# First block: the second gate's sums on ScalarE and GpSimd, and tile 0 normed, queried and routed ahead of tile 1

## What is computed

```python
mod = c_act @ w_ada[l] + b_ada[l]
shift1, scale1, gate1, shift2, scale2, gate2 = split(mod, 6)
h = rms_norm(x, norm1_g[l]) * (1 + scale1) + shift1
mix = concat(attention(h), conv(h), pool(h)) @ w_out[l]
x = x + gate1 * mix
h2 = rms_norm(x, norm2_g[l]) * (1 + scale2) + shift2
# peer_ffn(h2): 8 heads; q = h2 @ w_q; scores of 2 x 128 keys; top 16 of the sums;
# for each token and head 16 rows of peer_u and 16 rows of peer_v are gathered
x = x + gate2 * peer_ffn(h2, peer_wq[l], peer_keys[l], peer_u[l], peer_v[l])
```

## Time and profile before

| | us or share |
|---|---|
| median of three executions | 2767.92 |
| the profiled execution's own time | 2766.92 |
| its span in the profile | 2765.2 |
| TensorE matmul busy | 2401.3 (87%) |
| VectorE busy | 2048.1 (74%) |
| ScalarE busy | 770.8 (28%) |
| GpSimd busy | 1056.0 (38%) |
| bytes moved by DMA | 812.71 MB, mean 294 GB/s |

### The profile page before, as it was taken

One profiled execution on the slowest core, in us unless ns is written; L12 is line 12 of the kernel. 1 busy time (PEld: TensorE's weight loads), 2 busy tenths in 40 slices (PEclk: granted clock), 3 DMA queues, 4 the chain that ended last, 5 costly groups with the idle time before them and its releaser, 6 DMA issues. The chain is left out here.

```text
span 2765.2 us, 31596 instructions
## 1 busy us (share of the span) xinstructions
PE 2401.3 (87%) x9946; PEld 1612.3 (58%) x9946; DVE 2048.1 (74%) x3778; ACT 770.8 (28%) x1088; POOL 1056.0 (38%) x1144
## 2 busy tenths in 40 slices
PE   6979877787778989777778778999999999998998
PEld 5666333333335775333333336888878898887787
DVE  7877788787787876778778777667777656655765
ACT  3422011011012322101100114446543444345443
POOL 1336777777772336777777770002000000000000
PEclk9989998888889999999989889999999999999999
DMA  9789999999999789999999997664466655652564
GB/s 354 253 315 367 409 410 410 409 409 410 410 401 345 253 301 365 409 410 410 409 409 410 410 401 222 195 181 120 141 177 191 191 161 175 190 175 69 158 184 137
DMA packets 424192, 812.71 MB, mean 294 GB/s; under 512 B 26024, under 2 KB 262130, under 8 KB 424094
## 3 DMA queue, kind: packets, MB, share of 16 engines
q0 software_dynamic: 147968, 537.84, 49.2%
q1 hardware_dynamic: 276126, 273.62, 31.3%
HBM read 810.32 MB, written 1.05 MB: 293 GB/s over the span
## 5 line engine op out<-in xcount | busy, mean ns | idle before, releaser
L1833 PE MATMUL ps<-weight_ring,arena 128*128 128x512 f32 x1616 | 810.3, 661 | 254.6 <-PEq L1830 152.2
L1833 PEld LDWEIGHTS ps<-weight_ring,arena 128*128 128x128 f32 x1616 | 339.1, 214 | 720.6 <-issue 720.6
L2577 DVE CUSTOM_DVE_ANT_0 arena<-arena,ps 128x1024 f32<-128x1024 f32 x384 | 455.8, 1218 | 164.5 <-DMA arena<-in_peer_u,expert 145.4
L1466 PE MATMUL ps<-hT_pair,w_hi 128*128 128x512 f32 x1312 | 461.5, 396 | 7.4 <-PEq L1860 7.2
L2137 DVE TENSOR_TENSOR ring_lo<-weight_ring,w_hi 128x3072 fp32r<-128x3072 f32 (+1 forms) x102 | 325.4, 3191 | 172.0 <-DVEq L2136 171.9
L759 POOL DMA_INDIRECT weight_ring<-in_peer_v,expert x390 | 373.0, 956 | 121.2 <-issue 69.6
L753 POOL DMA_INDIRECT arena<-in_peer_u,expert x360 | 341.8, 949 | 134.9 <-issue 54.0
L1465 PE MATMUL ps<-hT_pair,ring_lo 128*128 128x256 f32 x1148 | 320.7, 279 | 0.0
L1466 PEld LDWEIGHTS ps<-hT_pair,w_hi 128*128 128x128 f32 x1312 | 240.8, 188 | 57.1 <-issue 10.1
L921 ACT ACTIVATE w_hi<-weight_ring 128x3072 fp32r<-128x3072 f32 (+1 forms) x102 | 267.7, 2626 | 8.8 <-ACTq L920 8.7
L1130 ACT ACTIVATE acts<-dots 128x8 f32<-128x8 f32 x64 | 13.2, 209 | 865.9 <-ACTq L1129 865.8
(11 more groups left out here) (404 smaller groups left out, 3943.6 us busy)
## 6 DMA issues: line engine op xcount, KB each, us to landing
weight_ring<-in_w_ada SPq DMA_DIRECT2D x48, 1024.0 KB, 7.5
weight_ring<-in_ffn_w_gate SPq DMA_DIRECT2D x88, 512.0 KB, 4.0
weight_ring<-in_ffn_w_up SPq DMA_DIRECT2D x88, 512.0 KB, 5.3
weight_ring<-in_ffn_w_down SPq DMA_DIRECT2D x88, 512.0 KB, 5.8
weight_ring<-in_peer_wq SPq DMA_DIRECT2D x16, 1024.0 KB, 9.6
weight_ring<-in_w_in SPq DMA_DIRECT2D x14, 1024.0 KB, 7.7
weight_ring<-in_rg_w_in SPq DMA_DIRECT2D x12, 896.0 KB, 5.2
weight_ring<-in_w_out SPq DMA_DIRECT2D x8, 1024.0 KB, 7.5
```

Of the source, the lines that this page charges most:

```text
L1466: ins = mm(both, w_high, s_pair, start=(k == 0), stop=last)
L1833: ins = mm(ps[:, 2 * t + c, :], diag[:, k, :], v_place(l, k)[:, c * N:(c + 1) * N], start=False, stop=False, skip_group_check=True)
L2577: ins = v.tensor_tensor_reduce(out=row, in0=row, in1=h_rows(t), scale=1.0, scalar=0.0, op0=ALU.mult, op1=ALU.add, accum_out=dots[:, g, j:j ...
```

## The change

- GATE2's eight partial sums leave VectorE. ScalarE scales the eight half pieces in place (Copy with a scale), GpSimd adds them up with eight `tensor_tensor` of 128x1024. GpSimd now raises `ada_free[q]` and `bias_free` of this segment. ScalarE's loop stands ahead of its copy of the spread SHIFT2.
- On VectorE tile 0 is added, normed and its head 0 routed (`best_pairs`) before tile 1 is added and normed. `next_first` goes 1 after `add_gated(0)`, 3 after tile 0's norm, 1 after `add_gated(1)`, 3 and 4 after tile 1's norm, 4 at the end. `slot_free[3]` is raised after `best_pairs(0)`.
- On TensorE `out_rows(3, 1)` moves behind `first_head(0)`; the spread of GATE2 waits for GpSimd; the spread of the next SCALE1 moves behind `query(1)`.
- On ScalarE tile 1's mean square moves behind `first_head(0)`, and writes its squares to `h` instead of the scratch `junk`.

```diff
--- before.py
+++ after.py
@@ -404,6 +404,8 @@
         gates_ready, root_in, root_ready = sem("gates_ready"), sem("root_in"), sem("root_ready")
         gelu_ready, rnn_out_ready = sem("gelu_ready"), sem("rnn_out_ready")
         wf_ready = sem("wf_ready")
+        gate2_in = [gates_ready, root_in, root_ready, gelu_ready]
+        gate2_bias_in, gate2_scaled, gate2_ready = rnn_out_ready, exp_ready, abs_ready
         zeroed_for_act = sem("zeroed_for_act")
         f_by_head, f_turned = qk_done, qk_turned
         f_ready, log_f_ready = sem("f_ready"), sem("log_f_ready")
@@ -482,8 +484,8 @@
                 sp.sem_inc(free, -1)
                 sp.dma_start(gain[:], A[name][l:l + 1].to_broadcast([P, D])).then_inc(given, 16)
 
-            def bias_row(l, segment, pad):
-                sp.dma_start(pad[0:1, :], A["b_ada"][l:l + 1, segment * D:(segment + 1) * D]).then_inc(bias_in, 16)
+            def bias_row(l, segment, pad, given=bias_in):
+                sp.dma_start(pad[0:1, :], A["b_ada"][l:l + 1, segment * D:(segment + 1) * D]).then_inc(given, 16)
 
             def segment_bias(l, segment):
                 sp.wait_ge(bias_free, 1)
@@ -552,9 +554,14 @@
                 segment_bias(l, SHIFT2)
                 for u in range(4):
                     later_piece(l, SHIFT2, u)
-                segment_bias(l, GATE2)
+                sp.wait_ge(bias_free, 1)
+                sp.sem_inc(bias_free, -1)
+                bias_row(l, GATE2, bias_pad, gate2_bias_in)
                 for q in range(ADA_PAIRS):
-                    later_piece(l, GATE2, q)
+                    sp.wait_ge(ada_free[q], 1)
+                    sp.sem_inc(ada_free[q], -1)
+                    src = A["w_ada"][l].rearrange("(p k) n -> p k n", k=KC)
+                    sp.dma_start(ada_piece(SLOTS + q), src[:, 2 * q:2 * q + 2, GATE2 * D:(GATE2 + 1) * D]).then_inc(gate2_in[q], 16)
                 w_q = of("peer_wq").rearrange("(k p) n -> p k n", p=P)
                 if l + 1 < DEPTH:
                     load_gain(l + 1, "norm1_g", gain_pre, pre_in, pre_free)
@@ -742,6 +749,22 @@
                     pool.wait_ge(pool_steps, steps.next())
                 pool.sem_inc(pool_steps, -steps.reset())
                 g.tensor_tensor(pooled[:], pooled[:], zc[:, 6:8, :], ALU.subtract).then_inc(pooled_ready, 1)
+
+                gate2 = mod[:, GATE2, :]
+                pool.wait_ge(gate2_bias_in, 16)
+                pool.sem_inc(gate2_bias_in, -16)
+                for q in range(ADA_PAIRS):
+                    for k in range(2):
+                        pool.wait_ge(gate2_scaled, 1)
+                        pool.sem_inc(gate2_scaled, -1)
+                        g.tensor_tensor(gate2, ada_piece(SLOTS + q)[:, k, :], bias_pad[:] if q == 0 and k == 0 else gate2,
+                                        ALU.add).then_inc(pool_steps, 1)
+                        pool.wait_ge(pool_steps, steps.next())
+                    pool.sem_inc(ada_free[q], 1)
+                    if q == 0:
+                        pool.sem_inc(bias_free, 1)
+                pool.sem_inc(gate2_ready, 1)
+                pool.sem_inc(pool_steps, -steps.reset())
 
 
                 chosen_by = [expert[:, 0, :], expert[:, 1, :], first_expert]
@@ -1065,11 +1088,15 @@
                 a.activation(mixT[:, 0:4, P:SEQ], ps[:, 2, :].rearrange("p (c t) -> p c t", t=P), ACT.Copy).then_inc(mixT_ready, 1)
                 a.activation(table_use[:], eps[:], ACT.Sqrt).then_inc(act_steps, 1)
                 act.wait_ge(act_steps, steps.next())
+                for q in range(ADA_PAIRS):
+                    act.wait_ge(gate2_in[q], 16)
+                    act.sem_inc(gate2_in[q], -16)
+                    for k in range(2):
+                        piece = ada_piece(SLOTS + q)[:, k, :]
+                        a.activation(piece, piece, ACT.Copy, scale=c_act[:, 2 * q + k:2 * q + k + 1]).then_inc(gate2_scaled, 1)
                 spread(mod[:, SHIFT2, :], 2)
                 norm_x_tile(0)
                 evacuate_hT_tile(0, hT, WORK)
-                norm_x_tile(1)
-                act.sem_inc(act_steps, -steps.reset())
 
                 def first_head(t):
 
@@ -1088,6 +1115,8 @@
                             fan(act, key_s_ready)
 
                 first_head(0)
+                norm_x_tile(1, h[:, 1, :])
+                act.sem_inc(act_steps, -steps.reset())
                 spread(mod[:, GATE2, :], 2)
                 evacuate_hT_tile(1, hT, WORK)
                 first_head(1)
@@ -1580,10 +1609,10 @@
                 pe.wait_ge(attn_done, 2)
                 pe.sem_inc(attn_done, -2)
 
-            def spread(source, bank, give, alone=True):
-
-                pe.wait_ge(segment_ready, 1)
-                pe.sem_inc(segment_ready, -1)
+            def spread(source, bank, give, alone=True, ready=segment_ready):
+
+                pe.wait_ge(ready, 1)
+                pe.sem_inc(ready, -1)
                 for c in range(2):
                     ins = mm(ps[:, bank + c, :], ones[:], source[:, c * N:(c + 1) * N], start=alone, stop=True)
                 ins.then_inc(give, 1)
@@ -1743,7 +1772,6 @@
                 out_rows(1, 1).then_inc(slot_free[1], 1)
                 spread(mod[:, SHIFT2, :], 2, spread_for_act)
                 out_rows(2, 1).then_inc(slot_free[2], 1)
-                out_rows(3, 1, stop=True)
 
                 def weights_in(head):
 
@@ -1777,11 +1805,10 @@
                 pe.sem_inc(spread_taken, -1)
                 w_first = weights_in(0)
                 first_head(0, w_first)
-                spread(mod[:, GATE2, :], 2, spread_for_act)
+                out_rows(3, 1, stop=True)
+                spread(mod[:, GATE2, :], 2, spread_for_act, ready=gate2_ready)
                 turn_h_tile(1, WORK)
                 first_head(1, w_first)
-                if l + 1 < DEPTH:
-                    spread(mod[:, 0, :], 6, spread_for_dve)
                 job = 4
 
                 def query(head):
@@ -1811,6 +1838,8 @@
                     job += 1
 
                 query(1)
+                if l + 1 < DEPTH:
+                    spread(mod[:, 0, :], 6, spread_for_dve)
                 for head in range(2, EXPERT_HEADS):
                     query(head)
                     key_products(head - 1)
@@ -2451,15 +2480,12 @@
                 while parts:
                     next_part()
                 more = l + 1 < DEPTH
-                later_part(0, mod[:, GATE2, :])
                 dve.wait_ge(post_in, 16)
                 dve.sem_inc(post_in, -16)
                 scaled_gain(mod[:, SCALE2, :], 0, gain_post[:])
                 dve.sem_inc(spread_taken, 1)
                 if l + 1 == DEPTH:
                     dve.sem_inc(post_free, 1)
-                for q in range(1, ADA_PAIRS):
-                    later_part(q, mod[:, GATE2, :])
                 take_mod()
                 first_parts = [(q, k, segment) for segment in (SCALE1, SHIFT1) for q in range(ADA_PAIRS) for k in range(2)] if more else []
 
@@ -2485,16 +2511,14 @@
                             if q == ADA_PAIRS - 1:
                                 dve.sem_inc(segment_ready, 1)
 
-                for t in range(TILES):
-                    dve.wait_ge(rows_done, 1)
-                    dve.sem_inc(rows_done, -1)
-                    if t == TILES - 1:
-                        dve.sem_inc(slot_free[SLOTS - 1], 1)
-                    add_gated(t, GATE1, h_rows)
-                    next_first(1)
-                    if t == 0:
-                        take_mod()
-                    normalise_tile(t, mod[:, SCALE2, :], mod[:, SHIFT2, :])
+                dve.wait_ge(rows_done, 1)
+                dve.sem_inc(rows_done, -1)
+                add_gated(0, GATE1, h_rows)
+                next_first(1)
+                take_mod()
+                normalise_tile(0, mod[:, SCALE2, :], mod[:, SHIFT2, :])
+                next_first(3)
+
                 def best_keys(s, scored=half_s):
 
                     v.max(best[:, s, 0:8], scored[:, s, :]).then_inc(dve_steps, 1)
@@ -2558,14 +2582,21 @@
                     head_scored()
                     best_keys(s, key_s[:, 0])
                 best_pairs(0, first_expert[:])
+                dve.wait_ge(rows_done, 1)
+                dve.sem_inc(rows_done, -1)
+                dve.sem_inc(slot_free[SLOTS - 1], 1)
+                add_gated(1, GATE1, h_rows)
+                next_first(1)
+                normalise_tile(1, mod[:, SCALE2, :], mod[:, SHIFT2, :])
                 if more:
-                    next_first(6)
+                    next_first(3)
+                    next_first(4)
                     dve.wait_ge(pre_in, 16)
                     dve.sem_inc(pre_in, -16)
                     scaled_gain(gain_pre[:], 6, gain_pre[:])
                     dve.sem_inc(spread_taken, 1)
                     dve.sem_inc(u_free, 1)
-                    next_first(8)
+                    next_first(4)
                     assert not first_parts
```

## The result

The kernel after took 2794.84 us (median of four executions, 2787.99 to 2797.32), beside 2770.22 for the kernel before (four executions, 2764.54 to 2775.84): a ratio of 1.0089, with a 95% interval from 1.0075 to 1.0102. It is slower by 24.6 us. The prediction was 2789, in a range from 2776 to 2797.

A forecast was written before the change was run, and what follows sets the result against it. The prediction took TensorE's row of queries, which opens the last gate before DMA saturates, as the bound. Layer 1's 15.4 plus layer 0's 5.6 made 21.0 us on 2766.92, 2787.9; the median runs 1.0 higher: 2789, range 2776 to 2797.

The forecast's parts named there:

- TensorE's row of queries: Claimed bound: query(1) plus the later heads' queries opens the last gate before DMA saturates, not the first gather.
- The rival that the first gather sets the end: The end moves with the first gather, -3.3 us at best in each layer: 2761, or 2768 if collisions eat it; chance 0.10.
- TensorE's two waits: Layer 0, heads 5 and 6: TensorE waited 1.13 us and about as much again; later queries needn't, 2.3 us less.
- the late case: Layer 0 with queries later than before: TensorE needn't wait for heads 5 and 6, 2.3 us less.
- Tile 0 in layer 1: Tile 0's norm ahead of tile 1 on VectorE: 3.3 us gained at best, 2.3 lost to collisions, a gain of 1.0.
- the collisions: GpSimd's adds and VectorE's two-input sums make each other wait while tile 0 is added and normed: 2.3 us lost.
- the 3.3: Layer 1: tile 0 normed at 976.05 us at the earliest, against 979.35, a gain of 3.3 us at best.
- Tile 0 in layer 0: The gain of 1.0 less 2.0 us of waiting for the next SCALE1's first piece: a loss of 1.0 us.
- Tile 1 behind the routing: Tile 1's uncovered chain delays query(1): 8.83 us from add_gated to first_head's first matmul, then 9.0 for first_head(1).
- The sum: Later queries cost +15.4 us in layer 1 and +5.6 in layer 0, 21.0 together: 2789.
- The loads behind slot_free[3]: Layer 0: weights of heads 6 and 7 land 5.2 us later than the gates allow: +26.3 us, 2794; chance 0.17.

The follow-up runs named there:

- the order alone: The kernel after, but with GATE2's eight sums left on VectorE, so only the order changes: 2790.43 us, ratio 1.0086 to the kernel before.
- the rows ahead: New order, GATE2's sums on VectorE, but tile 1's last output rows stay ahead of tile 0's turn on TensorE: 2789.46 us, ratio 1.0072 to kernel before.
- spread alone: The kernel before with only the spread of the next SCALE1 moved behind query(1), in layer 0: 2770.25 us, ratio 1.0002.

## Why the prediction was right, and where it was not

**What sets the end.** "The last gate opens by TensorE's row of queries" is shown for layer 1: by the table, and by the delayed query(1). The rival that the first gather sets the end fell there. For layer 0 it is true of the kernel after: TensorE had no wait for weights from query(1) to the last head, and h stands 57.62 us behind query(1), to 0.01 us as in the order alone and with the rows ahead. It is not true the other way round: queries earlier than those of the kernel before meet the loads and gain nothing (spread alone). The prediction saw TensorE's two waits there, but used them only for the late case. For a change that only made things later, that did no harm.

**Tile 0 in layer 1, forecast a gain of 1.0.** It is 0.0: the shifts end 32.8 us behind M in both kernels (979.35-946.60 and 984.69-951.90). The reciprocal starts 24.7 us behind M instead of 29.9, 5.2 earlier, not 3.3; but 1.7 of these 5.2 are the faster products right behind M (1.03+3.60 us, before 1.91+4.46), a matter of the clock in these two executions. Without them the gain ahead of the collisions is 3.5, near the 3.3, and tile 0 as a whole a loss of 1.7. The term that was undersized is the collisions, 5.2 instead of 2.3: scaling 2.35 instead of 1.28 and shifts 5.47 instead of 1.29. One GpSimd add takes 2.35 us when VectorE does nothing beside it, not the 2.05 of the prediction. The Trainium skill (GPSIMD Engine Reference, 3.1) gives about 2.6 cycles an element for a two-input add, and the prediction's estimate from it, 18.0 us for eight, is 2.25 for one. The trace agrees better with it than with my value. The Trainium skill (Perfetto Trace Analysis, Optimizing Scalar/DVE Operations) says that GpSimd and VectorE share a read port which "a 2-port DVE op" holds, so that moving work between them might not help. The trace agrees with the warning, and shows plain fp32 sums of two SBUF inputs among what meets there; the prediction read these words as leaving such sums out, and rightly priced by its rows.

**Tile 0 in layer 0, forecast a loss of 1.0.** It is 2.5 at the shifts (149.63, before 147.11). The piece of SCALE1 came at 141.73, a little ahead of the 142.48 that I took; scaling and shifts took 2.79 and 3.31 us. Of the 2.5 only 0.9 reached the first gather, since first_head(0) ran faster there (3.38+1.95 instead of 3.76+3.62), which is luck.

**Tile 1 behind the routing, forecast 8.83+9.0.** The mechanism is as forecast: the add starts at once behind the experts, TensorE idles 10 us, the clock falls to 0.50 and the queries wait. The chain from the add to the first product of the head took 9.54 us (1013.10-1003.56); the transposes at half clock were not in my 8.83. first_head(1) took 9.78 (1022.88-1013.10) instead of 9.0 in layer 1, and 7.85 in layer 0 (185.77-177.92).

**The sum.** Layer 0 was forecast at +5.6. query(1) came 6.2 us later (185.77), forecast 6.8; the row of queries lost its two waits, forecast 2.3, and is 2.2 shorter from query(1) to h; so h is 4.05 later. M moved by 5.3; the 1.3 in between is within what M - h scatters over the nine kernels. So layer 0 came out as summed, and for the reason that was given. Layer 1 was forecast at +15.4 for query(1). Behind M it is +18.55: the 1.0 of tile 0 that did not come, 0.8 more up to the first experts (51.4 us behind M, before 50.6), and 0.7 and 0.8 in the two chains; at an equal clock right behind M it would be 1.7 more. The gate behind head 7 of layer 1 was forecast at 1068.6 plus the shift of layer 0, 1074.2 us, and opened at 1077.06. The first product of the second block starts at 1706.02 instead of 1682.40, 23.6 us later, and this execution then took 2.6 us less for the second block (1080.2 us, before 1082.8), which the change doesn't touch. That the span grew by 21.0 us, exactly the forecast sum, is therefore in part chance: the first block lost 23.6.

**The loads behind slot_free[3].** This rival gives 2794, next to the median of 2794.84, but its mechanism was not seen: TensorE had no wait for weights between query(1) and the last key scores of layer 0 in the kernel after. The nearness is chance. The median lies above 2789 for two reasons that can be named: the four executions spread over 9 us, and layer 1 cost 3 us more than forecast.

**Not weighed:** the clock of first_head(0). It runs between 2.02+1.95 and 3.75+3.62 us from kernel to kernel, up to 3.4 us of the chain to the first experts, and I kept it as it was in each layer.

## What to carry to other kernels

Find the limit of each stage by itself, even where two stages run the same code: here layer 1 always followed its first query, while layer 0, which loads 8 MB more, followed its queries or the loads of the later heads' weights, whichever came last; and one edit can do opposite things to them. To find the limit, look for an event behind which the stage takes the same time in every variant, and distrust one that fits all variants but the kernel you started from. Before work is moved behind a step "to use the idle time", ask what the moved work feeds: tile 1's norm stood in covered time, and behind the routing nothing covered it. Work given to GpSimd to relieve VectorE is best run while VectorE has no operation with two SBUF inputs; here such operations paid for it.
